# Depthwise convolution of 31 taps: 32 channels laid four times on the partitions, four taps to a product, all taps on TensorE

## The reference

```python
def conformer_conv(h, w_pw1, b_pw1, w_dw, b_dw, ln_g, ln_b, w_pw2, b_pw2):
    u = h @ w_pw1 + b_pw1
    a, gate = jnp.split(u, 2, axis=-1)
    u = a * jax.nn.sigmoid(gate)
    u = lax.conv_general_dilated(          # y[t, c] = sum over 31 taps of w_dw[tap, c] * u[t - 30 + tap, c]
        u, w_dw[:, None, :].astype(u.dtype),
        window_strides=(1,), padding=((CONV_WIDTH - 1, 0),),
        dimension_numbers=("NWC", "WIO", "NWC"),
        feature_group_count=D_MODEL) + b_dw
    u = jax.nn.silu(layer_norm(u, ln_g, ln_b))
    return u @ w_pw2 + b_pw2
```

## Time and profile before

| what | value |
|---|---|
| median of 3 runs | 2129.07 us (2128.88 to 2129.3) |
| the profiled execution, its own time | 2130.01 us |
| its span in the trace | 2128.2 us |
| TensorE busy | 2047.7 us, 96% of the span |
| VectorE busy, ScalarE busy | 1533.0 us (72%), 1207.0 us (57%) |
| mean granted TensorE clock | 0.984 |
| stretch from the first pair to the mean | about 26.4 to 130.8 us |

### The profile page before, as it was taken

The page is one execution under the profiler, slowest core; times in us unless marked ns, Lnnn a source line. Parts: engine busy times, 40 slices in busy tenths (PEclk is TensorE's granted clock), DMA queues, the critical chain, the costliest instruction groups (busy, mean ns, idle before and its releaser), DMA issues.

```text
span 2128.2 us, 31732 instructions
## 1 busy us (share of the span) xinstructions
PE 2047.7 (96%) x12232; PEld 1801.2 (85%) x12232; DVE 1533.0 (72%) x1729; ACT 1207.0 (57%) x1357; POOL 52.6 (2%) x94
## 2 busy tenths in 40 slices
PE   7989999799999999999999999999999989999997
PEld 6979999687888888888878888889978869989997
DVE  5976562789898898888889898896576157626653
ACT  6554442467777676776777777675354246515442
POOL 2000000000000000000000000001000100020000
PEclk8999999799999999999999999999999989999999
DMA  4214444099898998989989898994432324444551
GB/s 190 80 71 168 179 178 159 29 348 362 326 354 337 345 370 314 366 337 344 346 338 366 326 354 337 347 368 150 179 139 93 128 77 159 159 159 170 187 179 60
DMA packets 70102, 504.19 MB, mean 237 GB/s; under 512 B 7680, under 2 KB 8704, under 8 KB 8832
## 3 DMA queue, kind: packets, MB, share of 16 engines
q1 hardware_dynamic: 70016, 502.95, 63.0%
HBM read 501.87 MB, written 1.05 MB: 236 GB/s over the span
## 4 chain that ended last, share of the span: by engine, by line
PE 86%; DVE 7%; ACT 4%; issue 2%; DMA 1%; POOL 0%; DVEq 0%; ACTq 0%; POOLq 0%; SPq 0%
PE ps L541 8%; PE ps L544 8%; PE ps L545 8%; PE ps L748 8%; PE ps L752 8%; PE ps L751 8%; PE ps L773 5%; PE ps L777 4%; PE ps L776 4%; PE ps L518 3%; PE ps L1033 2%; PE ps L602 2%; PE ps L1036 2%; PE ps L1035 2%; DVE ring_r L1693 2%
## 5 line engine op out<-in xcount | busy, mean ns | idle before, releaser
L1693 DVE TENSOR_TENSOR ring_r<-ring,high 128x2048 fp32r<-128x2048 f32 x227 | 517.6, 2288 | 98.2 <-ACT high L1351 92.3
L1351 ACT ACTIVATE high<-ring 128x2048 fp32r<-128x2048 f32 x224 | 428.5, 1913 | 16.5 <-DMA ring<-w_stream 16.4
L1559 DVE TENSOR_TENSOR ring_r<-ring,high 128x2048 fp32r<-128x2048 f32 x120 | 274.2, 2287 | 128.5 <-ACT high L1213 128.1
L751 PE MATMUL ps<-ring_r,big_r 128*128 128x512 f32 x896 | 349.0, 389 | 0.0
L544 PE MATMUL ps<-scr_r,high 128*128 128x256 f32 (+1 forms) x1200 | 344.2, 287 | 0.0
L1213 ACT ACTIVATE high<-ring 128x2048 fp32r<-128x2048 f32 x120 | 228.5, 1908 | 158.6 <-PE ps L541 87.9
L748 PE MATMUL ps<-high,big_r 128*128 128x512 f32 x704 | 288.1, 409 | 0.0
L752 PE MATMUL ps<-high,big_r 128*128 128x512 f32 x704 | 275.5, 391 | 0.0
L1693 DVE TENSOR_TENSOR ring_r<-ring,scr_r 128x2048 fp32r<-128x2048 f32 x112 | 254.8, 2287 | 5.6 <-ACT scr_r L1351 1.0
L541 PE MATMUL ps<-sq_r,high 128*128 128x272 f32 (+1 forms) x832 | 239.8, 288 | 7.6 <-DVE scr_r L1566 7.6
L545 PE MATMUL ps<-sq_r,ring_r 128*128 128x272 f32 (+1 forms) x832 | 238.7, 287 | 0.0
(11 more groups left out here) (405 smaller groups left out, 3793.7 us busy)
## 6 DMA issues: line engine op xcount, KB each, us to landing
ring<-w_stream SPq DMA_DIRECT2D x477, 1024.0 KB, 4.8
h<-h_in SPq DMA_DIRECT2D x1, 1088.0 KB, 5.1
out<-hn SPq DMA_DIRECT2D x1, 1024.0 KB, 4.7
vec<-vec_in SPq DMA_DIRECT2D x1, 576.0 KB, 8.0
```

Source lines behind the costliest of these rows:

```text
L751: pe.matmul(o, x_item_high[:, k, :], w_low[:, cols], start=False, stop=False)
L1351: act.activation(w_high, w, ACT.Copy).then_inc(S["moe_high"], 1)
L1559: dve.tensor_tensor(w_low, blocks_at(c, 0, CH), w_high.bitcast(F32), ALU.subtract).then_inc(S["weights_low"], 1)
L1693: dve.tensor_tensor(w_low, w, w_high.bitcast(F32), ALU.subtract).then_inc(S["moe_low"], 1)
```

## The change

Every tap moves to TensorE, and a product takes four taps. `conv_u` gets one more zero column behind the tokens (`CONV_LEN` 303), since 31 taps are filled up to 32 with a zero weight. For each tile and each group `g` of 32 channels, SyncE lays these 32 channels four times on the partitions, copy `s` shifted by `s` tokens: 4 x 4 DMAs from SBUF to SBUF, of [32 partitions, 300 tokens] each, into `shifted` (three buffers). The stationary matrix is [128, 32]: four diagonals of 32x32 under each other, one for each of four taps. Eight such products (`TAP_STEPS`), each four tokens further on, give the 32 taps of a group; the four groups write partitions 0 to 31, 32 to 63, 64 to 95 and 96 to 127 of bank 6. So a tile is 32 fp32 matmuls of 32 columns where it was 13 to 16 of 128.

The weights of a tile are laid out on the host as [128, 32] numbers, and VectorE makes all 32 stationary matrices of a tile with one instruction of [128, 1024] (`make_diag`); ScalarE's diagonals and `conv_dve` are gone. Instead VectorE moves the sum with the bias out of PSUM (`take_conv`). `conv_tile(j)` now follows pair `j + 2`. SyncE's chunks 6 to 17 are issued outside the loop, and the 16 DMAs of tile `j` stand behind chunk `6 + j`; each tile's DMAs wait for `glu_done` of the tile and for the landing of all DMAs of the tile before. The semaphore `h1_ready` is merged into `x_ready`, with counts shifted by 8.

```diff
-PE_TAPS = [13] * 6 + [15, 16]
+TURNS = 4
+GROUPS = P // 32
+TAP_STEPS = -(-CONVW // TURNS)
+CONV_PAD = TURNS * TAP_STEPS - CONVW
+CONV_LEN = CONVW - 1 + T0 + CONV_PAD
+SHIFT_LEN = T0 + TURNS * (TAP_STEPS - 1)
...
+            def shift(j):
+
+                sp.wait_ge(S["glu_done"], j + 1)
+                if j >= 3:
+                    sp.wait_ge(S["conv_done"], j - 2)
+                if j:
+                    sp.wait_ge(S["shift_landed"], 16 * GROUPS * TURNS * j)
+                for g in range(GROUPS):
+                    for s in range(TURNS):
+                        sp.dma_start(shifted[32 * s:32 * s + 32, j % 3, g, :],
+                                     conv_u[32 * g:32 * g + 32, j, s:s + SHIFT_LEN]).then_inc(S["shift_landed"], 16)
+
             turns_pre = C_MOE // RING
-            with sp.Fori(1, turns_pre) as r:
+            for c in range(RING, 3 * RING):
+                sp.wait_ge(pre_begun, c - RING + 2)
+                sp.dma_start(slot(c), w_stream[c]).then_inc(dense_landed[c % RING], 16)
+                if c - RING < KD - 1:
+                    shift(c - RING)
+                if c - RING == KD - 2:
+                    shift(KD - 1)
+            with sp.Fori(3, turns_pre) as r:
...
             def conv_tile(j):
-                pe.wait_ge(S["glu_done"], j + 1)
+                pe.wait_ge(S["shift_landed"], 16 * GROUPS * TURNS * (j + 1))
                 pe.wait_ge(S["diag_ready"], j + 1)
                 claim(6)
-                for tap in range(PE_TAPS[j]):
-                    mm = pe.matmul(ps[:, 6, 0:T0], diag[:, j % 2, tap, :], conv_u[:, j, tap:tap + T0],
-                                   start=(tap == 0), stop=(tap == PE_TAPS[j] - 1))
+                for n in range(TAP_STEPS):
+                    for g in range(GROUPS):
+                        mm = pe.matmul(ps[32 * g:32 * g + 32, 6, 0:T0], diag[:, j % 3, g * TAP_STEPS + n, :],
+                                       shifted[:, j % 3, g, TURNS * n:TURNS * n + T0],
+                                       start=(n == 0), stop=(n == TAP_STEPS - 1))
...
-                if j >= 1:
-                    conv_tile(j - 1)
                 if j >= 2:
-                    add_to_mean(j - 2)
+                    conv_tile(j - 2)
+                if j >= 3:
+                    add_to_mean(j - 3)
+            conv_tile(6)
+            add_to_mean(5)
             conv_tile(7)
             add_to_mean(6)
             add_to_mean(7)
...
-                for tap in range(PE_TAPS[j]):
-                    ins = act.activation(diag[:, j % 2, tap, :], ident[:, :], ACT.Copy,
-                                         scale=vcol("w_dw", j * CONVW + tap))
-                ins.then_inc(S["diag_ready"], 1)
...
-            def conv_dve(j):
...
+            step(dve.tensor_reduce(diagonal, ident[:, :].rearrange("p (b c) -> p c b", c=32), AX.X, ALU.add))
+
+            def make_diag(j):
+
+                if j >= 3:
+                    dve.wait_ge(S["conv_done"], j - 2)
+                n = GROUPS * TAP_STEPS
+                dve.tensor_tensor(diag[:, j % 3, :, :], diagonal.unsqueeze(1).broadcast_to([P, n, 32]),
+                                  vcol("w_dw", j * n, n).unsqueeze(2).broadcast_to([P, n, 32]), ALU.mult)\
+                   .then_inc(S["diag_ready"], 1)
+
+            def take_conv(j):
                 dve.wait_ge(S["conv_done"], j + 1)
+                dve.tensor_scalar(conv_y[:, j, :], ps[:, 6, 0:T0], vcol("b_dw", j), None, ALU.add)\
+                   .then_inc(S["conv_ready"], 1)
 
             for j in range(8):
                 split_weights((BOFF["pw1"] + j * KD + KD - 1) // CH + LOOK)
+                if j >= 3:
+                    take_conv(j - 3)
+                make_diag(j)
                 dve.wait_ge(S["glu_sig"], j + 1)
...
-                if j >= 1:
-                    conv_dve(j - 1)
-            conv_dve(7)
+            for j in range(5, 8):
+                take_conv(j)
```

More of the change, by code:

```diff
@@ L219, in vcol @@
             return vec[0:rows, VOFF[name] + j:VOFF[name] + j + n]
-        conv_u = big[:, 0:KD * 302].rearrange("p (k t) -> p k t", k=KD)
+        conv_u = big[:, 0:KD * CONV_LEN].rearrange("p (k t) -> p k t", k=KD)
         conv_y = big[:, 2432:2432 + KD * T0].rearrange("p (k t) -> p k t", k=KD)
-        diag = big[:, 4608:4608 + 2 * max(PE_TAPS) * P].rearrange("p (b t c) -> p b t c", b=2, c=P)
+        diag = big[:, 4608:4608 + 3 * GROUPS * TAP_STEPS * 32].rearrange("p (b n c) -> p b n c", b=3, c=32)
+        shifted = big[:, 7680:7680 + 3 * GROUPS * SHIFT_LEN].rearrange("p (b g t) -> p b g t", b=3, g=GROUPS)
+        diagonal = scr[:, 4352:4384]
         pool_a = big[:, 6000:6000 + 2 * T0].rearrange("p (k t) -> p k t", k=2)
@@ L254, in program @@
         mean = gate_sb[:, 0, :]
-        conv_sum = up_sb[:, 0, :]
         zo = proj[:, 0:8, :]
@@ L631, in _ @@
                            after_split(1) if j == 0 else None)
-                bank_owner[b] = (S["h1_ready"], 2 * j + 1)
-                bank_owner[b + 1] = (S["h1_ready"], 2 * j + 2)
+                bank_owner[b] = (S["x_ready"], 2 * j + 1)
+                bank_owner[b + 1] = (S["x_ready"], 2 * j + 2)
             def ffn(n, norm_i, split_n, t, x_low, hidden_high, hidden_low, b_in, b_out):
@@ L668, in _ @@
                 pair(BOFF["pool"] + 2 * g, 2, lambda k: sq256[:, 2 * g + k, :], SEQ, b, S["pool_done"])
-                bank_owner[b] = (S["x_ready"], 2 * g + 1)
-                bank_owner[b + 1] = (S["x_ready"], 2 * g + 2)
+                bank_owner[b] = (S["x_ready"], KD + 2 * g + 1)
+                bank_owner[b + 1] = (S["x_ready"], KD + 2 * g + 2)
                 if g:
@@ L682, in turn_tokens @@
                 mm.then_inc(S["xt_done"], 1)
-            pe.wait_ge(S["x_ready"], 8)
+            pe.wait_ge(S["x_ready"], KD + 8)
             turn_tokens(0)
@@ L1283, in _ @@
                     for k in (2 * j - 2, 2 * j - 1):
-                        act.wait_ge(S["h1_ready"], k + 1)
+                        act.wait_ge(S["x_ready"], k + 1)
                         act.activation(sq_r[:, k, :], h[:, k, :], ACT.Copy, scale=vcol("ffn_g0", k))\
@@ L1314, in _ @@
             for k in range(KD):
-                act.wait_ge(S["x_ready"], k + 1)
+                act.wait_ge(S["x_ready"], KD + k + 1)
                 act.activation(hn[:, k, 0:SEQ], x[:, k, :], ACT.Copy, scale=vcol("ffn_g1", k))\
@@ L1590, in norm @@
                         low_part(low[:, k - 1, 0:t], dst[:, k - 1, 0:t], sq_r[:, k - 1, 0:t], "input_low")
-            step(dve.memset(conv_u[:, :, 0:CONVW - 1], 0.0))
+            dve.memset(conv_u[:, :, 0:CONVW - 1], 0.0)
+            step(dve.memset(conv_u[:, :, CONVW - 1 + T0:], 0.0))
             dve.wait_ge(S["h_landed"], 16)
@@ L1596, in _ @@
             dve.wait_ge(S["consts_ready"], 1)
-            def conv_dve(j):
[L1600 to L1615, removed]
+            step(dve.tensor_reduce(diagonal, ident[:, :].rearrange("p (b c) -> p c b", c=32), AX.X, ALU.add))
[7 more added lines that the diff above has]
+            def take_conv(j):
                 dve.wait_ge(S["conv_done"], j + 1)
-                dve.scalar_tensor_tensor(out=conv_y[:, j, :], in0=ps[:, 6, 0:T0], scalar=vcol("b_dw", j),
-                                         in1=conv_sum, op0=ALU.add, op1=ALU.add).then_inc(S["conv_ready"], 1)
-                dve.wait_ge(S["conv_ready"], j + 1)
+                dve.tensor_scalar(conv_y[:, j, :], ps[:, 6, 0:T0], vcol("b_dw", j), None, ALU.add)\
+                   .then_inc(S["conv_ready"], 1)
             for j in range(8):
                 split_weights((BOFF["pw1"] + j * KD + KD - 1) // CH + LOOK)
+                if j >= 3:
+                    take_conv(j - 3)
+                make_diag(j)
                 dve.wait_ge(S["glu_sig"], j + 1)
@@ L1647, in _ @@
                                              scalar=vcol("b_pw2", m), in1=h[:, m, :], op0=ALU.add, op1=ALU.add)\
-                       .then_inc(S["h1_ready"], 1)
+                       .then_inc(S["x_ready"], 1)
                 if j:
@@ L2327, in taps, with turned_taps @@
         return w.reshape(w.shape[0], -1, P).transpose(2, 1, 0).reshape(P, -1)
+    def turned_taps(w):
+        w = np.concatenate([w, np.zeros((CONV_PAD, D), w.dtype)]).reshape(TAP_STEPS, TURNS, KD, GROUPS, 32)
+        return w.transpose(1, 4, 2, 3, 0).reshape(P, -1)
     def tall(v):
@@ L2337, in _kernel_arrays @@
     vecs = {
-        "b_pw1": cols(a["conv_b_pw1"][0]), "w_dw": taps(a["conv_w_dw"][0]), "b_dw": cols(a["conv_b_dw"][0]),
+        "b_pw1": cols(a["conv_b_pw1"][0]), "w_dw": turned_taps(a["conv_w_dw"][0]), "b_dw": cols(a["conv_b_dw"][0]),
         "ln_g": cols(a["conv_ln_g"][0]), "ln_b": cols(a["conv_ln_b"][0]), "b_pw2": cols(a["conv_b_pw2"][0]),
```

7 lines of the change are left out of this document (3 added, 4 removed).

## The result

| kernel | median us (lowest to highest, runs) | ratio to before [95% interval] |
|---|---|---|
| before | 2129.19 (2128.88 to 2130.33, 4) | 1 |
| after | 2148.92 (2145.98 to 2150.42, 4) | 1.0088 [1.0075, 1.0102] |

The change makes the kernel slower, by 19.7 us. Forecast was 2116.6, in a range of 2110 to 2139. The profiled execution of after took 2147.47 us, its span is 2145.6, and the mean granted clock 0.981.

The account below looks back on a forecast made before the run. TensorE was taken to bound, with a 17.6 us tail of engines waiting in turn. The copy of the mean 14.5 us earlier, plus 2.0 for the clock, gave -12.5: 2117.5 profiled, 2116.6 median, range 2110 to 2139.

Parts of the forecast that it names:

- a tile's time on TensorE: Convolution on TensorE: 64 records, four groups at a time, 3.7 us and shape changes, 3.87 for a tile.
- my bound of 7.4 for two at a time: Rival for TensorE's convolution tiles: only two groups overlap, 7.4 us a tile, +10 us, 2139; chance 0.09.
- The turn was 10.3 by forecast: TensorE's steady turn in the convolution: 6.17 + 3.87 + 0.27 = 10.3 us, against 12.4 before.
- VectorE's part, the start, the landing: VectorE's matrices 1.14 us a tile; SyncE starts tile 0 at 36.9; a copy lands in 1.8 us, bounds 1.0 and 5.0.
- I take 0.49: SyncE's step between copy issues: 0.49 us, bounds 0.40 and 0.55, making 9.25 us for a tile.
- the "third": SyncE's issue step could be above 0.55 by a third if small copies from SBUF are dearer.
- the 118.3 that they give for the copy of the mean: End of the convolution: mean copied at 116.3 instead of 130.81, 14.5 us less, before 2 us for the clock.
- the clock: TensorE's tile 7, after a 5 us wait, runs partly at 1.2 GHz: 2 us lost, between 0 and 3.9.
- SyncE becomes the bound outright: Rival: SyncE's chain of 128 issues and landings bounds; at step 0.65, +6.7, 2136; step above 0.62 or late landings: 0.11.
- its own formula, 59.5 + 120 p: SyncE rival's end of the convolution for a step p between issues; 125.5 at p of 0.55.
- its point of decision, 0.594: SyncE rival: from a step of 0.594 us between issues the change loses.
- all that follows have the same instructions and the same waits: Layer norm and all stages behind the convolution keep instructions and waits; no time was added for them.

Follow-up runs that it names:

- the two kernels in which TensorE bounds: After with four 128-partition copies a tile instead of 16: 2118.02 us; after with three semaphores, two issuing engines, ScalarE's split first, vec 1216 wide: 2109.97 us.
- the run with the groups outside: Against after, the two loops of conv_tile exchanged, all eight steps of one group before the next group: 2193.37 us (one run).
- The four copies: Against after, 4 copies of 128 partitions for each tile instead of 16 of 32, convolution values wrong: 2118.02 us, ratio 0.9947.
- the two issuers (with the loop cut): Against after: three semaphores, ScalarE issues groups 2 and 3 of tile j - 1 behind its next split, vec 1216 wide: 2109.97 us, ratio 0.9906.

## Why the prediction was wrong, point by point

**Held: a tile's time on TensorE.** Forecast 3.87 us, and four strips at a time. The group of the new product between 0 and 170 us (out<-in, shapes, count; busy us, mean ns; idle before):

```profile
L629 PE MATMUL ps<-big 128*32 128x272 f32 x512 | 37.8, 457 | 25.1 <-DMA big<-big 25.1
```

At the full clock a tile's 64 records take 3.80 to 3.88 us, 0.06 for each where a single strip needs 0.230, and they start in fours. Against my bound of 7.4 for two at a time this leaves no doubt. The turn was 10.3 by forecast, and 10.46 and 10.47 in the two kernels in which TensorE bounds. The reading of the earlier trace rows was right that a later strip can pass three waiting records, and the run with the groups outside shows that it is not more. The Trainium skill (TensorE: Matmul & The Clock Gate, Part 3, The mechanism) has matmuls in strict program order; 3.8 us for a tile in which the two records of a matmul stand together disagrees with it, and so does the record at 71.676 above, which starts ahead of three that stand before it in the program.

**Held: VectorE's part, the start, the landing.** The matrices of a tile step by 1.14 us (34.02 in the chain), as said. SyncE starts at 35.59, 1.3 earlier than forecast, since the second split ended at 34.02 instead of 35.15; 0.15 of it is a slip of the sum, since 35.56 + 1.14 is 36.70 and not 36.85. The landing is 1.9, against 1.8. That was in part luck: the 1.8 came from the two ends of a 1 MB load, with bounds from 1.0 to 5.0.

**Failed: "I take 0.49" for SyncE's step between issues.** It is 0.633, above the 0.40 to 0.55 of the rows and inside the "third" that was left for dearer copies. The earlier trace rows show the issues of large loads; I took the value from them and the size of the copy for a reason to be cheaper. The cost goes neither with bytes nor with partitions: copies four times as large have about the same, and even the 1 MB chunk's issue takes 0.58 behind the copies. Why an issue steps by 0.633 here and by 0.47 to 0.55 at the start was not isolated. The terms of the prediction, from the 118.3 that they give for the copy of the mean (116.3 and 2 for the clock) to the 140.4 measured:
- start 35.6 instead of 36.9: -1.3
- 8 x 15 steps at 0.143 more: +17.2
- long issues and late landings (1.1 to 1.6 us now and then, a landing of 3.56 behind a chunk at 104.67), which the sum had not: +5.2, so that 35.6 to 132.0 is 96.4 where 74.0 stood
- tile 7 with the tail, 8.4 instead of 7.4: +1.0, of which 0.6 is the clock and 0.4 that two additions to the mean stand behind tile 7 (1.37 us at 138.44)

The rival "SyncE becomes the bound outright" is what happened; its own formula, 59.5 + 120 p, gives 135.5 at 0.633, and its point of decision, 0.594, lies below the measured step. It had a chance of 0.11. The four copies and the two issuers (with the loop cut) show it by removing the cause in two ways: the mean goes to 109.6 and 111.0, earlier than forecast, with TensorE's part unchanged.

**Held in kind: the clock.** Forecast were 2 us on tile 7. Four windows of after: an idle stretch, tile 6, the second idle stretch, tile 7 (columns as above, the granted clock is third from the end):

```profile
112.80:119.60 6.80, 0.00 (x0) 0.00 (x0) 0.00 (x0) 0.00 (x0) 0.00 (x0) 0.79 0.21 58
119.70:125.40 5.70, 5.70 (x65) 2.48 (x65) 0.00 (x0) 0.00 (x0) 0.00 (x0) 0.66 0.21 50
126.10:132.00 5.90, 0.00 (x0) 0.00 (x0) 0.00 (x0) 0.00 (x0) 0.00 (x0) 0.86 0.24 59
132.00:138.40 6.40, 6.39 (x65) 2.77 (x65) 0.00 (x0) 0.00 (x0) 0.00 (x0) 0.59 0.00 0
```

1.00 is the level of 2.4 GHz and 0.50 that of 1.2 GHz; a value between them is the mean of a window that has both. Behind the first idle wait tile 6 runs at a mean of 0.66, and behind the second tile 7 at 0.59, mostly at the lower level; they take 5.8 and 6.43 us instead of 3.87. Tile 7 lost 2.6, against the 2 forecast. Tiles 0 and 6 lost as well (6.21 and 5.8 us), but on a path that SyncE bounds, only tile 7's counts.

**Failed: "all that follows have the same instructions and the same waits".** True, and not enough. The instructions are the same, but one tensor's width moved the addresses, and 10.9 of the 19.7 us are that. Nothing in the working looked at it; it stood in the sum as zero. With SyncE's step at 0.49 the sum and this term would have given about 2127.5 (2116.6 + 10.9), an estimate. With the step right and nothing else, the rival's formula gives 135.5 for the mean, or about 2134; the long issues, the late landings and the tail, which it had not, bring that to the 2138.06 measured with the addresses of before modulo 256 bytes. That value would lie inside the range that was stated, but on the side of slower, so the sign was missed by the step alone.

## What to carry to other kernels

Count the DMA issues of each queue, not their bytes, and hold turns of the issuing engine against turns of the engine that it feeds: 16 small copies cost 10 us of one queue. With the addresses put right, a semaphore for each buffer and the copies split over two queues, behind the issuing engine's urgent work and not ahead of it, moved the ratio to before from 1.0041 to 0.9906. When a change alters the size of any tensor in SBUF, run the kernel before with the same shift of addresses alone, or fill it up to the old place modulo 256 bytes, before reading anything into the time. A helper that a loop of four engines passes through (a split, a gate) must not stand behind issues on any of them.

## What the runs showed of the hardware

- An issue behind another issue of SBUF-to-SBUF copies steps 0.633 us, with 32 or 128 partitions, and about as much on ScalarE's queue while SyncE issues too (medians of 0.643 and 0.637 with two issuers). In the kernels with 128 copies 3 to 8 of them took 0.94 to 1.94 us. The large loads of the earlier trace rows stepped 0.47 to 0.55, and one behind copies takes 0.58.
- 32 bytes on the place of the tensors behind `vec` cost 6 ns on each 512-column product of the experts (0.227 to 0.233), at the full clock and with no wait between, and gave 1 ns on the late products of 256 columns (0.119 to 0.118); 64 bytes cost the experts 9.5 us in place of 12.1, 256 nothing. What is served more slowly is open. The weights that come through `ring_r` and `high` did not move, the tokens in `big_r` did; that they are the cause was not isolated.
- Four column strips of 32 run at a time in fp32: 64 records of 272 columns in 3.80 us, which singly need 14.7. A strip's record passes three waiting ones of another strip, not more: with the strips one behind the other a tile takes 12.19 us.
